# A hybrid gMLP / HGRN2 layer on one core: the start of the work buffers in SBUF is rounded differently

## The reference

```python
h_lat = modulate(rms_norm(x, norm1_gain[layer]), sh1, sc1)
h_ctx = modulate(rms_norm(ctx, norm1_gain[layer]), csh1, csc1)
mix_lat, mix_ctx = token_mixer(h_lat, h_ctx, w_in[layer], ...)   # gMLP group A, HGRN2 scans group B
x = x + g1[:, None, :] * (mix_lat @ w_out[layer])
h = modulate(rms_norm(x, norm2_gain[layer]), sh2, sc2)
x = x + g2[:, None, :] * squared_relu_mlp(h, w_ff1[layer], w_ff2[layer])
return rms_norm(x, final_gain)
```

## Time and profile before

| what | value |
|---|---|
| median of 3 runs | 2719.71 us (2717.97 to 2720.36) |
| the profiled execution, its own time | 2719.71 us |
| its span, first to last instruction | 2717.8 us |
| PE busy | 2563.4 us, 94% |
| DVE busy | 1246.9 us, 46% |
| POOL busy | 1000.9 us, 37% |
| ACT busy | 727.6 us, 27% |
| mean granted TensorE clock | 0.979 of full |

### The profile page before, as it was taken

One profiled execution on the slowest core, in us unless ns is written; L12 is line 12 of the kernel. 1 busy time (PEld: TensorE's weight loads), 2 busy tenths in 40 slices (PEclk: granted clock), 3 DMA queues, 4 the chain that ended last, 5 costly groups with the idle time before them and its releaser, 6 DMA issues.

```text
span 2717.8 us, 33317 instructions
## 1 busy us (share of the span) xinstructions
PE 2563.4 (94%) x12240; PEld 2111.8 (78%) x12240; DVE 1246.9 (46%) x1463; ACT 727.6 (27%) x929; POOL 1000.9 (37%) x420
## 2 busy tenths in 40 slices
PE   4789999999999999998899999999999999999997
PEld 0479787777777887787788888888888888888886
DVE  0476447788888523666423223332332333323224
ACT  1344222222222223223321322212222222231222
POOL 0330243323232343343344444444444444444442
PEclk9899999999999999999999999999999999999998
DMA  9734454333443452364133323232322322232322
GB/s 411 279 121 163 165 192 150 131 123 123 134 144 124 141 208 93 114 229 153 62 101 109 101 93 102 93 101 94 99 96 97 98 94 100 94 101 93 102 93 101
DMA packets 104769, 354.70 MB, mean 131 GB/s; under 512 B 9936, under 2 KB 10192, under 8 KB 100688
## 3 DMA queue, kind: packets, MB, share of 16 engines
q1 hardware_dynamic: 104224, 352.46, 38.1%
q10 hardware_dynamic: 432, 0.54, 0.1%
HBM read 348.77 MB, written 4.19 MB: 130 GB/s over the span
## 4 chain that ended last, share of the span: by engine, by line
PE 55%; issue 29%; POOL 10%; DMA 3%; DVE 2%; ACT 1%; POOLq 0%; SPq 0%; DVEq 0%; ACTq 0%
POOL w_lo L313 10%; PE bank L1108 9%; PE bank L1109 9%; PE bank L1110 9%; PE bank L1122 9%; PE bank L1123 9%; PE bank L1124 9%; DMA ada_w<-in_w_ada 3%; DVE prep_tmp L669 0%; DVE x_tok L659 0%; DVE x_res L1056 0%; PE bank L1068 0%; ACT junk L393 0%; DVE g_tmp L1034 0%; PE bank L1157 0%
## 5 line engine op out<-in xcount | busy, mean ns | idle before, releaser
L313 POOL TENSOR_TENSOR w_lo<-raw,w_hi 128x1024 fp32r<-128x1024 f32 x416 | 1000.7, 2406 | 1691.7 <-ACT w_hi L346 1691.7
L346 ACT ACTIVATE w_hi<-raw 128x1024 fp32r<-128x1024 f32 x448 | 475.5, 1062 | 1681.4 <-PE bank L1110 870.9
L1108 PE MATMUL bank<-h_hi,w_hi 128*128 128x512 f32 x1696 | 673.6, 397 | 3.4 <-POOL w_lo L313 2.9
L1109 PE MATMUL bank<-h_lo,w_hi 128*128 128x512 f32 x1696 | 663.7, 391 | 0.0
L1110 PE MATMUL bank<-h_hi,w_lo 128*128 128x512 f32 x1696 | 663.6, 391 | 0.0
L1122 PE MATMUL bank<-w_hi,hid_hi 128*128 128x512 f32 x1024 | 398.3, 389 | 0.0
L1123 PE MATMUL bank<-w_lo,hid_hi 128*128 128x512 f32 x1024 | 398.3, 389 | 0.0
L1124 PE MATMUL bank<-w_hi,hid_lo 128*128 128x512 f32 x1024 | 398.3, 389 | 0.0
L1108 PEld LDWEIGHTS bank<-h_hi,w_hi 128*128 128x128 f32 x1696 | 321.1, 189 | 69.8 <-POOL w_lo L313 3.4
L1110 PEld LDWEIGHTS bank<-h_hi,w_lo 128*128 128x128 f32 x1696 | 320.4, 189 | 68.0
L1109 PEld LDWEIGHTS bank<-h_lo,w_hi 128*128 128x128 f32 x1696 | 321.2, 189 | 63.6
(11 more groups left out here) (182 smaller groups left out, 2089.0 us busy)
## 6 DMA issues: line engine op xcount, KB each, us to landing
raw<-in_w_stream SPq DMA_DIRECT2D x448, 512.0 KB, 3.5
ada_w<-in_w_ada SPq DMA_DIRECT2D x128, 512.0 KB, 4.1
ada_w<-in_w_ada SPq DMA_DIRECT2D x16, 2048.0 KB, 18.0
x_tok<-in_x SPq DMA_DIRECT2D x4, 1024.0 KB, 27.1
x_res<-in_x SPq DMA_DIRECT2D x4, 1024.0 KB, 12.1
out<-x_res SPq DMA_DIRECT2D x4, 1024.0 KB, 4.0
ctx_tok<-in_ctx_x SPq DMA_DIRECT2D x2, 1024.0 KB, 16.5
fin_row<-in_final_row SPq DMA_DIRECT2D x1, 1024.0 KB, 7.0
```

Source lines behind the costliest of these rows:

```text
L313: pool.tensor_tensor(w_lo[:, r % 2], raw[:, r], w_hi[:, r % 2].bitcast(F32), ALU.subtract).then_inc(lo_done, 1)
L346: act.activation(w_hi[:, r % 2], raw[:, r], ACT.Copy).then_inc(hi_done, 1)
L1108: pe.matmul(dst, wh, hi[:, kt], start=(kt == 0), stop=False)
L1109: pe.matmul(dst, wh, lo[:, kt], start=False, stop=False)
```

## The change

The diff is whole:

```diff
@@ -69,7 +69,7 @@
-        where = [base + (-base) % P]
+        where = [base + (-base) % 32]
@@ -111,7 +111,7 @@
         lbl = fixed("lbl", [P, 2, 2 * HEADS])
-        w0 = where[0] + (-where[0]) % P
+        w0 = where[0]
         assert w0 + 108 * KB <= top, (w0, top)
```

## The result

The changed kernel takes 2738.64 us in the median of 4 runs (2733.56 to 2742.68), against 2719.65 us before, also 4 runs: 19.0 us slower. The ratio on record, with 13 executions of the changed kernel, is 1.0074, interval 1.006 to 1.0086. The forecast was no change, 2719.7 us, with a range to 2727. It was wrong.

What follows compares the result with a forecast made beforehand. PE was taken to bound the kernel, busy 2563.4 of 2717.8 us and without slack in the MLP. To 2719.71 us every term added 0, giving 2719.7 us, with a range from 2715.5 to 2727 us.

Steps and rivals of the forecast that it cites:

- The first edit: Buffers of `fixed`: worth nothing, since byte 16481 rounds up to 16512 with either divisor, so they stay.
- the term for DVE, ACT and transfers: Their moved buffers: 0 each; bounds 2.4 us either way plus 0.2 us in the tail, transfers 0 to 2 us.
- PE, MLP. Term: 0, and from 0 to 0 in the range: MLP `wide` units: 3072 weight loads from moved hid_hi and hid_lo were to cost nothing, with no allowance in the range.
- The contention rival: DVE copies beside POOL's instructions: the shift dissolves a contention by place modulo 128, 18 us faster, 2701.6 us; chance 0.05.
- the cover: MLP: a load growing from 0.11 to 0.138 us stays hidden beside a 0.227 us matmul, 0.09 us to spare.
- PE pays for crooked operands: Rival, context heads and score products: operands off a multiple of 128 cost 23.8 us, 2743.5 us; chance 0.07.
- 0 to 84 us: MLP weight loads: 84 us was the price of 3072 loads at 0.0275 us each if they were not covered.

Runs made afterwards that it cites:

- after_hid_back: The changed kernel with only hid_hi and hid_lo put back at their addresses of before; 2719.47 us, ratio 0.9997.
- all_96: The kernel before with every buffer, weights and activations too, starting 96 bytes higher; 2720.45 us, ratio 1.0001.
- dose_128_384: The kernel before with hid_hi 128 and hid_lo 384 bytes higher, all else in place; 2736.26 us, ratio 1.0053.
- hid_lo_128: The kernel before with hid_lo alone 128 bytes higher; 2730.58 us, ratio 1.0042.
- dose_32_64: The kernel before with hid_hi 32 and hid_lo 64 bytes higher; 2731.30 us in one run.

## Why the prediction was wrong

**The first edit and the term for DVE, ACT and transfers: right.** No `fixed` buffer moved. (The prediction has the modulation for the first norm stay as a whole; its stationary operand `cs_wide` is a work buffer and moved, but PE waits for the loads there, 51.6 us before and 51.0 after.) The medians of the copies, PE's wait for `q_meet` and the landing of `ada_w` are those of before, and `after_hid_back` shows with a tight interval (0.9987 to 1.0006) that all work buffers but two can stand 96 past a multiple of 128 at no cost.

**"PE, MLP. Term: 0, and from 0 to 0 in the range": this is the step that failed.** It measured 18.5 to 18.9 us. Two things in it were wrong. The first is the question. I asked whether the start of an operand is crooked, and priced a longer read of it. The runs show that a start off a multiple of 128 can be free (`all_96`) and one on a multiple can be dear (`dose_128_384`): what the change broke was the distance between two buffers, -32 instead of 0 modulo 256. The section on the change says it, "their distances to `raw`, `w_hi`, `w_lo`, `h_hi` and `h_lo` are 32 bytes less", and the sum had no term for it. The contention rival spoke of places relative to each other, but between DVE and POOL, and only as a gain.

The second is the cover. I argued that a load may grow from 0.11 to 0.138 us unseen, because it lies beside a matmul of 0.227 us. That holds for a load that only gets longer. But the record of the load kept its length (188 ns before, 187 after), and it was the matmul that got longer, of which PE has 100% in this stretch. `hid_lo_128` and `dose_32_64` show that the load beside a matmul has a part in it. Nor did the spacings show that "the load adds nothing": I subtracted 0.12 from 0.227 us, and a cost that both have drops out of the difference. Each has some 13 or 14 ns over its columns, and in the changed kernel the 512-column ones have 20. What these 14 ns consist of no run here shows.

**"PE pays for crooked operands": near in its number, 2743.5 us, by luck, and wrong in its place.** It laid the price on the 256-column matmuls (11.5 us) and the score products (12.3 us), which pay nothing, 281 and 275 ns, and left out the MLP, which pays nearly all.

**The width.** The only exact bound of the range, 0 to 0, stood at the term with the most instructions on the full engine: 3072 matmuls, where each ns is 3.1 us. A cost that no row shows, in a stretch without any slack, should have had both ends. With 0 to 84 us, the number that I worked out beside it, the range would have held the time.

The Trainium skill's page "SBUF — State Buffer", section "SBUF: two separate sides", says that on the engines' side only the port pair shared by VectorE and GpSimd causes contention, and that PE never waits on anyone. Nothing here contradicts it as to other engines: 389 ns were measured with DVE, ACT and POOL busy as ever. But by that rule the addresses of PE's operands would not matter, and in these runs they are worth up to 8 ns per matmul.

## What to carry to other kernels

When buffers move, list which pairs of operands meet in one instruction and how the distance between the two changes; an alignment that looks like mere tidiness may be what keeps such a distance. In this kernel stationary and moving operands of 512-column float32r matmuls should start at the same place modulo 256 bytes; two such places were tried, 128 and 224 past a multiple of 256, and they are equally good. For matmuls of 256 columns the runs show no such need. And where an engine is busy 100% of a stretch, a term of zero per instruction needs a bound before it is multiplied by thousands.

## What the runs showed of the hardware

- The spacing of 512-column float32r matmuls, each with its own weight load, is 0.227 us if the starts of stationary and moving operand are equal modulo 256 bytes (shifts of 0, 256 and 512 bytes measured), and 0.228 to 0.235 us otherwise (7 other values of D; least at 32 and 192, most at 96).
- Groups of matmuls with the same D have the same spacing, whichever operand holds the weights: 233.2 to 233.4 ns in three groups at D = 64.
- A common shift of all buffers by 96 bytes changed nothing: ratio 1.0001, interval 0.9991 to 1.0011.
- The weight-load records stay at 187 to 188 ns while the matmuls beside them go from 227 to 233 ns apart. Where only the load beside it had another distance (line 1123 in `hid_lo_128`), a matmul paid that distance's price.
- Matmuls of 256 columns were 120 ns apart at D = 0 and 118 ns at D = 32, and those of 128 columns had 275 ns where both operands moved together: no loss in either.
